# Which of three streams of expert blocks ends in an unfilled step

## The chip, the core and the metric

The kernel runs on one core of one Trainium2 chip. The metric is the device time of one execution in microseconds, here the median of three runs. A profile is one more execution, taken with the hardware profiler on; its span runs from the first instruction to the last.

## The reference, cut to what matters

Two transformer blocks are computed for 512 tokens of width 1024, in float32. The second one ends in a mixture of 32 experts (4 groups of 8). Each token picks its group and the best two experts in it, so there are 1024 assignments of a token to an expert. All of them, whatever their number for one expert, go through that expert's three matrices of 1024x512, 1024x512 and 512x1024:

```python
def hierarchical_moe(h, rg_w, rg_b, re_w, re_b, w_gate, w_up, w_down):
...
    grp = jnp.argmax(group_logits, axis=-1).astype(jnp.int32)
...
    top_val, top_idx = lax.top_k(in_group, TOP_K)
    gate = p_grp * jax.nn.softmax(top_val, axis=-1)
    expert_id = grp[:, None] * EXPERTS_PER_GROUP + top_idx.astype(jnp.int32)
...
    def expert_block(args):
        xb, e = args
        a = xb @ w_gate[e]
        u = xb @ w_up[e]
        return (jax.nn.silu(a) * u) @ w_down[e]
```

The results of a token's two experts are added to it with their gates as weights, and a last normalisation follows.

## The kernel before

The first 1495 us or so are dense layers, attention and a recurrent mixer, and the change touches nothing of them. The router follows, then the experts, then the final gathering and normalisation.

**Blocks and steps.** An expert's assignments are cut into blocks of 32 rows (`BS`). The work on the experts is a chain of steps, one block in each. TensorE does for step c: the gate and up products (`gate_up`, L1760), the transposes of the next step's rows (`next_rows`, L1678), the down product of step c-1 (`down`, L1778) and the transposes of its own products (`turn_products`, L1786). ScalarE and VectorE do the copies and the SiLU in between, GpSimd gathers the rows of later steps, and ScalarE's queue stores each result to `y_rows`.

**Three streams.** Step c belongs to stream c % 3 (`SETS` is 3), and each stream has its own place in SBUF for the three matrices of one expert (`sets`), 3 x 2048 KB. Three steps, one of each stream, are a lap. The number of laps is worked out on the chip, from the routing, and every engine reads it into a register (`laps`). Below, steps count from 0, laps from 0, and the streams are called first, second and third. With the inputs of this case there are 54 steps in 18 laps.

**When weights are loaded.** All loads of weights are issued from SyncE's queue in order of the steps: gate and up of step c once TensorE has ended the gate and up products of step c-3 (`load_first`), and down of step c-1 once the down product of step c-4 is done (`load_down`). A load is conditional (`cond=needed`, L923): the table `need` holds 0 where the stream's next step has the same expert as its last one, and where the step is not filled. So a stream that stays with one expert loads nothing, and an unfilled step loads nothing, though its products are computed all the same, on whatever the buffers hold. Steps 0 to 2 use the experts 0, 1 and 2, whose matrices are loaded before the routing is known.

**How blocks are placed.** The other 29 experts are put in a row, those with the most blocks first, and this row is laid along the first stream from its position 1 to its end, then along the second and then the third. On VectorE this is a sum: `place` is three times the position in that row (`quota` holds the expert's start, `rdiv` the block within the expert), so it is right for the first stream; where it is `turn` or more (three times the number of laps, 54), `shift[:, 0:1]` is added, which moves it into the second stream; where it is `past` or more, `shift[:, 1:2]` is added too, for the third. `heads` holds the blocks of the experts 0, 1 and 2, at least 1 each, `total` all blocks with these, here 53. What is left of the 54 steps is then at the end of the third stream.

**Blocks of this case.** By the reference on the inputs, experts 0 and 1 have one block each and expert 2 none (it still has its step). Of the others, two have 5 blocks, one has 4, two have 3, seven have 2 and sixteen have 1, together 50. So the row is laid like this, each number one expert's blocks, and | the step of the heads:

```
first  stream:  1 | 5 5 4 3                  (17 positions)
second stream:  1 | 3 2 2 2 2 2 2 2          (17)
third  stream:  0 | 1 x 16, and one unfilled (17)
```

The sets of three matrices that laps 1 to 17 load are then 3, 1, 1, 2, 1, 3, 1, 2, 1, 2, 2, 2, 1, 2, 2, 2, 0, together 28. The issues in the trace show this step by step: a transfer that is made takes SyncE's queue 0.33 us or more to issue, one that is left out 0.07 to 0.09 us.

Of the kernel before, what the change touches and what calls it, by code (L numbers as in the profile page):

```python
# [35 lines left out]
SETS = 3  # L36
# [8 lines left out]
ACT, ALU, AX = mybir.ActivationFunctionType, mybir.AluOpType, mybir.AxisListType  # L45
# [83 lines left out]
def build(nc, x_d, cols_d, rows_d, wdense_d, wff_d, wif_d, wr_d, strips_d, experts_d, out_d):  # L129
# [3 lines left out]
    DV = Queue("dv", nc.vector, sem("dve_steps"))  # L133
    PO = Queue("po", nc.gpsimd, sem("pool_steps"))
    SP = Queue("sp", nc.sync, None)
    pe, ac, dv, po, sp = nc.tensor, nc.scalar, nc.vector, nc.gpsimd, nc.sync
# [14 lines left out]
    def sb(name, words, dt=F32, parts=128):  # L151
        return nc.alloc_sbuf_tensor(name, [parts, words], dt)
# [34 lines left out]
    def sm(n):  # L187
        a = small_at[0]
        small_at[0] += n
        assert small_at[0] <= SMALL  # L190
        return small[:, a:a + n]
# [26 lines left out]
    iota_f, tok_id, fold = sb("iota_f", 128), sm(2 * NT), sm(2 * BS)  # L218
# [831 lines left out]
    place = ((2, 0), (3, 0), (2, 0), (3, 384))  # L1050
# [459 lines left out]
    DV.step(dv.tensor_copy(quota[:, 0:3], iota_f[:, 0:3]))  # L1510
    nb, numbers = sm(33), sm(33)
    DV.step(dv.memset(nb[:, 32:33], 0.0))
    DV.step(dv.tensor_copy(numbers[:, 0:32], iota_f[:, 0:32]))
    DV.step(dv.tensor_scalar(numbers[:, 32:33], tok_id[:, 0:1], float(NO_ROW), None, ALU.add))
    DV.step(dv.tensor_scalar(multiples, iota_f[:, 1:T // BS], float(BS), None, ALU.mult))
# [60 lines left out]
    heads, ids1, key, ahead = sm(3), sm(C2), sm(33), sm(1)  # L1576
    pair, total, most, rest, turn = sm(1), sm(1), sm(1), sm(1), sm(1)
    shift, past = sm(2), sm(1)
# [24 lines left out]
    DV.run(dv.tensor_scalar(turn, turn, most, None, ALU.max))  # L1603
    counted_laps = DV.step(dv.tensor_scalar(rest.bitcast(I32), turn, -1.0, None, ALU.add))
    DV.run(dv.tensor_scalar(turn, turn, float(SETS), None, ALU.mult))
    DV.run(dv.tensor_scalar(shift, shift, turn, None, ALU.subtract))
    DV.step(dv.scalar_tensor_tensor(past, turn, 1.0, shift[:, 0:1], ALU.add, ALU.subtract))

    chosen = work[:, 0:2 * NT * 32]
    rank, rdiv, rmod = sm(C2), sm(C2), sm(C2)  # L1610
    place, late, posf, pos = sm(C2), sm(C2), sm(C2), sm(C2)
# [12 lines left out]
                            quota.unsqueeze(1).to_broadcast([128, C2, 32]), ALU.mult))  # L1624
    DV.run(dv.tensor_reduce(place, chosen.rearrange("p (c e) -> p c e", e=32), axis=AX.X, op=ALU.add))
    DV.run(dv.scalar_tensor_tensor(place, rdiv, float(SETS), place, ALU.mult, ALU.add))
    DV.step(dv.tensor_scalar(late, place, turn, shift[:, 0:1], ALU.is_ge, ALU.mult))
    DV.run(dv.tensor_scalar(posf, place, past, shift[:, 1:2], ALU.is_ge, ALU.mult))
    DV.run(dv.tensor_tensor(late, late, posf, ALU.add))
    DV.run(dv.tensor_tensor(place, place, late, ALU.add))  # L1630
# [438 lines left out]
```

How the kernel before makes its waits and increments, by code:

```python
    def run(self, ins):  # L114
        s = self.step(ins)
        self.eng.wait_ge(self.sem, s.value(self.loop))
        return s
# [1 line left out]
    def wait(self, *steps):  # L120
        for s in steps:
            if s is not None:
                self.eng.wait_ge(s.queue.sem, s.value(self.loop))
# [5 lines left out]
def build(nc, x_d, cols_d, rows_d, wdense_d, wff_d, wif_d, wr_d, strips_d, experts_d, out_d):  # L129
# [77 lines left out]
    cleared = PO.run(po.memset(zeros, 0.0))  # L207
    PO.run(po.affine_select(out=ident[:, :], in_=ident[:, :], compare_op=ALU.not_equal, fill=1.0, base=0,
                            pattern=[[-1, 128]], channel_multiplier=1))
    PO.run(po.affine_select(out=tri[:, :], in_=ones[:, :], compare_op=ALU.is_ge, fill=0.0, base=0,
                            pattern=[[1, 128]], channel_multiplier=-1))
    c_ready = PO.run(po.affine_select(out=tri_strict[:, :], in_=ones[:, :], compare_op=ALU.is_gt, fill=0.0,
                                      base=0, pattern=[[1, 128]], channel_multiplier=-1))
    for q in (PE, AC, DV):
        q.wait(c_ready)
        q.eng.wait_ge(s_cols, 16)
    iota_f, tok_id, fold = sb("iota_f", 128), sm(2 * NT), sm(2 * BS)
    PO.run(po.tensor_tensor(fold, ident[:, 0:2 * BS], ident[:, 2 * BS:4 * BS], ALU.add))
    PO.run(po.iota(iota_f[:, :].bitcast(I32), [[1, 128]], base=0, channel_multiplier=0))
# [272 lines left out]
    for k in range(KD):  # L493
        if k % 2 == 0:
            ac.wait_ge(s_x[k // 2], 16)
            dv.wait_ge(s_x[k // 2], 16)
# [32 lines left out]
    dv.wait_ge(s_strip, 16)
    for hh in range(12):
```

## Time and profile before

| | us |
|---|---|
| median of 3 runs | 2052.38 |
| lowest and highest | 2051.47, 2054.06 |
| the profiled execution | 2054.98 |
| its span | 2053.7 |
| SyncE's first conditional load of weights | 1527.21 |
| first loads for step 5 issued (end of lap 0) | 1539.66 |
| first loads for step 53 issued (end of lap 16) | 1994.00 |
| end of the last down product | 2020.33 |

TensorE is busy for 89% of the span. In the stretch of the experts the page's row for the DMA engines is at 9 tenths in slices 31 to 38, with 374 to 415 GB/s, where it stands at 2 or 3 tenths for most of the time before. The laps are cut here at the moment when SyncE issues the first loads for the third stream's next step, which is when TensorE has ended the third stream's gate and up products of that lap. Such a lap lasts 21.2 us where nothing waits, 7.07 us for a step.

### The profile page before, as it was taken

The page shows a single profiled execution, that of the slowest core. Times are in us where ns is not written, and L with a number is a line of the kernel's source. Part 1 is how long each engine was busy: PE and PEld are TensorE (multiplying, and loading weights), DVE is VectorE, ACT ScalarE, POOL GpSimd, SP SyncE. Part 2 cuts the span into 40 slices and gives each one's busy share as a digit, 9 for nine tenths or more (in the row PEclk, how much of TensorE's full clock was granted, in tenths as well). Part 3 has the DMA queues.
Part 4 walks back from the last instruction along what each step waited for, and adds up shares of the span by engine and source line. Part 5 has one row for each costly group of instructions (what it writes and reads, how often), then busy time and mean ns, then how long its engine had stood idle before and what let it go on. Part 6 is the DMA issues. An engine that isn't in the chain of part 4 may idle for free.

```text
span 2053.7 us, 27415 instructions
## 1 busy us (share of the span) xinstructions
PE 1824.7 (89%) x9686; PEld 1287.1 (63%) x9686; DVE 863.6 (42%) x1256; ACT 432.7 (21%) x794; POOL 992.7 (48%) x536
## 2 busy tenths in 40 slices
PE   5999999989999899999999798996877978969783
PEld 4888888877776578888888666664642423323331
DVE  5444443410254567444444489877341111111113
ACT  3111100100244432111100143551321211111112
POOL 5888887767544278888888523321211111101101
PEclk9999999999999999999999999997868988988897
DMA  3333363423221123333333222210579999999983
GB/s 126 97 97 93 105 262 98 141 79 98 66 62 52 32 85 95 97 93 101 92 109 98 72 60 64 72 52 21 212 287 412 374 408 402 410 415 398 413 358 133
DMA packets 56977, 346.00 MB, mean 168 GB/s; under 512 B 8474, under 2 KB 8858, under 8 KB 44896
## 3 DMA queue, kind: packets, MB, share of 16 engines
q1 hardware_dynamic: 44640, 315.12, 42.1%
q10 hardware_dynamic: 7968, 19.46, 2.6%
q0 software_dynamic: 4320, 10.78, 1.5%
q8 instruction: 29, 0.48, 0.1%
q14 instruction: 20, 0.16, 0.0%
HBM read 475.06 MB, written 19.66 MB: 241 GB/s over the span
## 4 chain that ended last, share of the span: by engine, by line
PE 70%; DMA 13%; DVE 11%; ACT 3%; issue 1%; POOL 1%; SPq 0%; DVEq 0%; ACTq 0%; POOLq 0%
PE bank L460 31%; DMA big<-w_up_in 13%; PE bank L431 12%; PE bank L1760 7%; PE bank L692 4%; PE bank L1266 3%; DVE big L1043 3%; PE bank L1778 2%; PE bank L479 2%; PE bank L1376 2%; PE bank L1786 1%; PE bank L610 1%; DVE state L1028 1%; PE bank L670 1%; PE bank L1678 1%
## 5 line engine op out<-in xcount | busy, mean ns | idle before, releaser
L277 POOL TENSOR_TENSOR weights_hi_parts<-ring,ones 128x1024 fp32r<-128x1024 f32 (+1 forms) x176 | 356.6, 2026 | 304.7 <-PE bank L460 139.1
L279 POOL TENSOR_TENSOR ring_parts<-ring,weights_hi_parts 128x1024 fp32r<-128x1024 f32 (+1 forms) x176 | 473.9, 2693 | 13.8
L460 PE MATMUL bank<-attention_buffers_parts,weights_hi_parts 128*128 128x512 f32 x832 | 329.4, 396 | 27.9 <-POOL ring_parts L279 17.6
L460 PE MATMUL bank<-state_parts,weights_hi_parts 128*128 128x512 f32 x832 | 326.8, 393 | 0.0
L460 PE MATMUL bank<-attention_buffers_parts,ring_parts 128*128 128x512 f32 x832 | 326.7, 393 | 0.0
L1760 PE MATMUL bank<-big,work 128*32 128x512 f32 x1440 | 231.7, 685 | 54.5 <-DMA big<-w_up_in 54.4
L431 PE MATMUL bank<-big_parts,weights_hi_parts 128*128 128x512 f32 x704 | 217.1, 389 | 1.2 <-POOL ring_parts L279 1.2
L460 PEld LDWEIGHTS bank<-attention_buffers_parts,weights_hi_parts 128*128 128x128 f32 x832 | 158.1, 190 | 64.6 <-POOL ring_parts L279 17.6
L864 POOL TENSOR_TENSOR ring_parts<-ring,weights_hi_parts 128x1024 fp32r<-128x1024 f32 x32 | 81.0, 2534 | 234.1 <-ACT weights_hi_parts L861 234.1
L1860 POOL TENSOR_TENSOR small<-small 128x1 f32<-128x1 f32 x51 | 9.7, 190 | 381.3 <-DVE small L1683 381.3
L460 PEld LDWEIGHTS bank<-state_parts,weights_hi_parts 128*128 128x128 f32 x832 | 158.3, 190 | 33.4 <-issue 0.8
L460 PEld LDWEIGHTS bank<-attention_buffers_parts,ring_parts 128*128 128x128 f32 x832 | 158.0, 190 | 33.5
L1719 DVE TENSOR_TENSOR work<-bank,cols 128x256 f32<-128x256 f32 x54 | 22.9, 425 | 306.0 <-PE bank L1678 304.9
L431 PEld LDWEIGHTS bank<-big_parts,weights_hi_parts 128*128 128x128 f32 x704 | 132.0, 188 | 29.2 <-POOL ring_parts L279 2.0
L1760 PEld LDWEIGHTS bank<-big,work 128*32 128x32 f32 x1440 | 63.6, 123 | 135.3 <-issue 129.6
L431 PE MATMUL bank<-big_parts,ring_parts 128*128 128x512 f32 x352 | 136.9, 389 | 0.0
L406 DVE TENSOR_TENSOR work<-bank,token_scale 128x512 f32<-128x512 f32 x44 | 30.4, 692 | 199.9 <-PE bank L460 199.9
L1043 DVE SCALAR_TENSOR_TENSOR big<-big,cols 128x512 f32<-128x512 f32 x120 | 106.5, 929 | 6.4 <-ACT big L1037 5.3
L315 DVE TENSOR_TENSOR big_parts<-work,big_parts 128x512 f32 (+1 forms) x44 | 82.9, 1884 | 42.3 <-ACT big_parts L313 42.3
L1792 ACT ACTIVATE weights_hi<-bank 128x512 f32<-128x512 f32 x54 | 32.3, 598 | 312.1 <-PE bank L1760 312.1
L1760 PE MATMUL bank<-attention_buffers,work 128*32 128x512 f32 x288 | 75.0, 667 | 24.0 <-DMA big<-w_up_in 23.4
L313 ACT ACTIVATE big_parts<-work 128x512 f32 (+1 forms) x44 | 27.9, 633 | 287.3 <-DVE work L408 287.3
(377 smaller groups left out, 2827.1 us busy)
## 6 DMA issues: line engine op xcount, KB each, us to landing
big<-w_up_in SPq DMA_DIRECT2D x54, 2048.0 KB
ring<-wdense_in SPq DMA_DIRECT2D x176, 512.0 KB, 3.6
state<-w_down_in SPq DMA_DIRECT2D x37, 2048.0 KB
big<-w_gate_in SPq DMA_DIRECT2D x36, 2048.0 KB
attention_buffers<-w_gate_in SPq DMA_DIRECT2D x18, 2048.0 KB
ring<-w_down_in SPq DMA_DIRECT2D x18, 2048.0 KB
ring<-wff_in SPq DMA_DIRECT2D x32, 704.0 KB, 4.1
y_rows<-big ACTq DMA_DIRECT2D x1, 8192.0 KB, 28.0
```

The costliest lines, as they stand in the source:

```text
L277: po.tensor_tensor(hi, raw, ones[:, 0:1].to_broadcast([128, words]), ALU.mult).then_inc(PO.sem, 1)
L279: po.tensor_tensor(lo, raw, hi.bitcast(F32), ALU.subtract) \
L315: return DV.step(dv.tensor_tensor(lo, raw, hi.bitcast(F32), ALU.subtract))
L431: m = pe.matmul(bank, x, y_, start=t + k + n == 0, stop=t == 1 and k == h - 1 and n == 2)
L460: m = pe.matmul(out, x, y_, start=j + n == 0, stop=j == len(pairs) - 1 and n == len(ts) - 1)
L479: m = pe.matmul(banks[t][:, :], x, y_, start=k + n == 0, stop=k == KD - 1 and n == len(ts) - 1)
L692: m = pe.matmul(banks[7][:, :], x, y_, start=k + t == 0, stop=k == KD - 1 and t == 2, skip_group_check=True)
L864: lo_made[n] = PO.step(po.tensor_tensor(lo, raw, hi.bitcast(F32), ALU.subtract))
L1043: last = DV.step(dv.scalar_tensor_tensor(dst, src, w, dst, ALU.mult, ALU.add))
L1266: m = pe.matmul(banks[bank][:, :], x, y_, start=k + j == 0, stop=k == KD - 1 and j == 2, skip_group_check=True)
L1376: m = pe.matmul(bank[:, :], x, y_, start=k == 4 and n == 0, stop=k == 3 and n == 2, skip_group_check=True)
L1760: m = pe.matmul(first_products[b][p:p + BS, :], xet[:, (k + odd) * BS:(k + odd + 1) * BS], sets[b][m_][:, (k + odd) * D_EXP:(k + odd + 1) ...
```

## The change

One step of the row, or two, that no block fills are moved: with one unfilled step it is the last of the first stream, and with two they are the last of the first and of the second. Before they were the last of the third. `room` holds three times the number of positions that the first and the second stream have, and takes the place of `turn` in `shift`, `past` and `late`. `spare` is a new constant (1, 2), which becomes 1 or 0 for "at least one (two) unfilled". `room` is never less than three times the blocks of that stream's head.

```diff
@@ -1510,6 +1510,8 @@
     DV.step(dv.memset(nb[:, 32:33], 0.0))
+    spare, room = sm(2), sm(2)
+    DV.step(dv.tensor_copy(spare, iota_f[:, 1:3]))
     DV.step(dv.tensor_copy(numbers[:, 0:32], iota_f[:, 0:32]))
@@ -1603,8 +1605,12 @@
     DV.run(dv.tensor_scalar(turn, turn, float(SETS), None, ALU.mult))
-    DV.run(dv.tensor_scalar(shift, shift, turn, None, ALU.subtract))
-    DV.step(dv.scalar_tensor_tensor(past, turn, 1.0, shift[:, 0:1], ALU.add, ALU.subtract))
+
+    DV.run(dv.tensor_scalar(spare, spare, total, turn, ALU.add, ALU.is_le))
+    DV.run(dv.tensor_scalar(spare, spare, -float(SETS), turn, ALU.mult, ALU.add))
+    DV.run(dv.scalar_tensor_tensor(room, heads[:, 0:2], float(SETS), spare, ALU.mult, ALU.max))
+    DV.run(dv.tensor_tensor(shift, shift, room, ALU.subtract))
+    DV.step(dv.scalar_tensor_tensor(past, room[:, 1:2], 1.0, shift[:, 0:1], ALU.add, ALU.subtract))
@@ -1624,7 +1630,7 @@
-    DV.step(dv.tensor_scalar(late, place, turn, shift[:, 0:1], ALU.is_ge, ALU.mult))
+    DV.step(dv.tensor_scalar(late, place, room[:, 0:1], shift[:, 0:1], ALU.is_ge, ALU.mult))
```

`run` is a step after which the engine waits for its end; `step` has no such wait. On VectorE, in the routing, the kernel before has these rows, where `small` is the buffer in which `turn`, `shift`, `past` and `rest` are columns:

```order
 L1603 TENSOR_SCALAR small<-small 128x1
 L1604 TENSOR_SCALAR small<-small 128x1
 L1605 TENSOR_SCALAR small<-small 128x1
 L1606 TENSOR_SCALAR small<-small 128x2
 L1607 SCALAR_TENSOR_TENSOR small<-small 128x1
 L1614 TENSOR_TENSOR work<-small,bank 128x256
```

and the changed kernel has these in the same place:

```order
 L1605 TENSOR_SCALAR small<-small 128x1
 L1606 TENSOR_SCALAR small<-small 128x1
 L1607 TENSOR_SCALAR small<-small 128x1
 L1609 TENSOR_SCALAR small<-small 128x2
 L1610 TENSOR_SCALAR small<-small 128x2
 L1611 SCALAR_TENSOR_TENSOR small<-small 128x2
 L1612 TENSOR_TENSOR small<-small 128x2
 L1613 SCALAR_TENSOR_TENSOR small<-small 128x1
 L1620 TENSOR_TENSOR work<-small,bank 128x256
```

Three small operations have come in between the number of laps and the placing of the blocks. The copy for `spare` (L1514) stands earlier, among the constants. No other engine has a row more or less, or in another place: the loops are the same, and what differs in them is the contents of the tables (which expert and which rows a step has, and which loads are left out).

## Rows read from the trace of the kernel before

**Rows 1.** The page, the span in 40 slices: gigabytes per second moved by DMA.
```profile
GB/s 126 97 97 93 105 262 98 141 79 98 66 62 52 32 85 95 97 93 101 92 109 98 72 60 64 72 52 21 212 287 412 374 408 402 410 415 398 413 358 133
```
**Rows 2.** SyncE's queue: start, duration, line, what it loads, times.
```profile
1967.38 0.33 SPq L923 DMA_DIRECT2D big<-w_gate_in  x1
...
1974.45 0.09 SPq L923 DMA_DIRECT2D attention_buffers<-w_gate_in  x1
...
1976.91 0.34 SPq L923 DMA_DIRECT2D state<-w_down_in  x1
...
1994.00 0.07 SPq L923 DMA_DIRECT2D big<-w_gate_in  x1
```
**Rows 3.** Windows, laps 1 to 14, one row each; columns in the first line.
```profile
core 0: us, PE busy (x) PEld busy (x) DVE busy (x) ACT busy (x) POOL busy (x), PEclk, DMA share, GB/s
1539.66:1580.57 40.91, 26.23 (x195) 10.71 (x194) 4.24 (x12) 4.41 (x10) 3.31 (x6) 0.79 1.01 415
1580.57:1601.78 21.21, 21.21 (x195) 8.68 (x194) 4.24 (x12) 4.41 (x10) 3.34 (x6) 1.00 0.93 359
1601.78:1622.98 21.20, 21.20 (x195) 8.67 (x194) 4.24 (x12) 4.41 (x10) 3.31 (x6) 1.00 0.96 368
1622.98:1650.03 27.05, 22.86 (x195) 9.96 (x194) 4.24 (x12) 4.41 (x10) 3.34 (x6) 0.94 1.02 414
1650.03:1671.23 21.20, 21.20 (x195) 8.66 (x194) 4.24 (x12) 4.40 (x10) 3.31 (x6) 1.00 1.01 400
1671.23:1716.79 45.56, 27.95 (x195) 11.40 (x194) 4.23 (x12) 4.41 (x10) 3.34 (x6) 0.74 1.01 417
1716.79:1738.00 21.21, 21.21 (x195) 8.68 (x194) 4.24 (x12) 4.41 (x10) 3.31 (x6) 1.00 0.98 377
1738.00:1765.48 27.48, 23.09 (x195) 9.91 (x194) 4.24 (x12) 4.41 (x10) 3.34 (x6) 0.94 1.01 413
1765.48:1786.69 21.21, 21.21 (x195) 8.68 (x194) 4.23 (x12) 4.41 (x10) 3.31 (x6) 1.00 1.01 410
1786.69:1815.88 29.19, 24.01 (x195) 9.53 (x194) 4.24 (x12) 4.40 (x10) 3.34 (x6) 0.88 1.01 410
1815.88:1853.47 37.59, 26.91 (x195) 9.96 (x194) 4.24 (x12) 4.41 (x10) 3.31 (x6) 0.77 1.01 415
1853.47:1880.48 27.01, 24.20 (x195) 9.34 (x194) 4.23 (x12) 4.40 (x10) 3.34 (x6) 0.87 0.99 411
1880.48:1901.69 21.21, 21.21 (x195) 8.67 (x194) 4.24 (x12) 4.41 (x10) 3.31 (x6) 1.00 0.97 377
1901.69:1929.78 28.09, 24.68 (x195) 10.69 (x194) 4.24 (x12) 4.40 (x10) 3.34 (x6) 0.88 1.01 410
```
**Rows 4.** TensorE's timeline: start, duration, line, operation, times, the idle time before it.
```profile
1644.78 4.93 PE L1760 MATMUL bank<-big,work 128*32 128x512 f32 x32 [4.10 <-DMA big<-w_up_in]
...
1988.36 5.34 PE L1760 MATMUL bank<-big,work 128*32 128x512 f32 x32 [3.23 <-DMA big<-w_up_in]
...
2011.26 3.64 PE L1760 MATMUL bank<-big,work 128*32 128x512 f32 x32
...
2018.41 1.92 PE L1778 MATMUL bank<-state,weights_hi 128*32 128x512 f32 x16 [0.76 <-DVE weights_hi L1830]
```
**Rows 5.** Windows where the transfers end, columns as in rows 3.
```profile
1992.00:1994.00 2.00, 2.00 (x22) 0.69 (x15) 0.00 (x0) 0.25 (x1) 0.00 (x0) 0.95 1.02 434
1994.00:1995.00 1.00, 1.00 (x13) 0.48 (x16) 0.47 (x2) 0.35 (x1) 0.00 (x0) 1.00 0.43 180
1995.00:1996.00 1.00, 1.00 (x12) 0.13 (x4) 0.00 (x0) 0.00 (x0) 0.00 (x0) 1.00 0.16 66
```
**Rows 6.** VectorE's timeline in the routing: start, duration, line, operation, form.
```profile
1506.61 0.27 DVE L1597 TENSOR_SCALAR small<-small 128x1 f32<-128x1 f32 x1
...
1507.87 0.14 DVE L1605 TENSOR_SCALAR small<-small 128x1 f32<-128x1 f32 x1
1508.05 0.23 DVE L1606 TENSOR_SCALAR small<-small 128x2 f32<-128x2 f32 x1
1508.31 0.16 DVE L1607 SCALAR_TENSOR_TENSOR small<-small 128x1 f32<-128x1 f32 x1
```

## The prediction, made before the changed kernel ran

> **What bounds the kernel now.** I read the page's slices first: in slices 31 to 38 DMA moves 374 to 415 GB/s, against mostly 60 to 110 before [rows 1]. That is where the experts run, so the question is whether TensorE or the transfers set the pace there. The windows cut at laps answer it [rows 3]. In a lap with one set of weights TensorE is busy for all of its 21.2 us at a granted clock of 1.00. In a lap with two or three sets it is not (22.9 to 28.0 us busy of 27.0 to 45.6), its clock falls to 0.74 to 0.94, and DMA moves 410 to 417 GB/s with a share of about 1. The timeline of TensorE shows the waits: a step's gate and up products start after an idle time that the landing of `w_up` ends [rows 4]. So the bound is the transfers, in all laps but those with one set, and even there 359 to 410 GB/s flow, of what earlier laps left over. A set is 3 x 2048 KB = 6.29 MB, 15.2 us at 415 GB/s. Besides it a lap moves 0.8 MB of gathered rows and stored results (3 x 0.13 MB each way), 1.9 us.
>
> **What the change does to the sets.** The unfilled step exists: at 1994.00 the loads for step 53 are left out (0.07 us), where those of steps that load take 0.33 us and more [rows 2]. It goes to step 51. The first stream then holds 16 positions after its head, 5 5 4 2; the second 17, 1 3 2 2 2 2 2 2 1; the third 17, 1 and 1 x 16. Before, the two boundaries between streams fell between experts. Now one expert with three blocks and one with two are cut in two, and each is loaded in both streams. Sets in laps 1 to 17:
>
> before: 3 1 1 2 1 3 1 2 1 2 2 2 1 2 2 2 0, together 28
> after: 3 2 1 1 2 2 2 1 2 1 3 1 2 1 3 1 2, together 30
>
> Two costs and one gain follow: 12.6 MB more through a full queue, and a last step that has to wait for its weights; but the weights now end with the last step instead of three steps before it.
>
> **Sum by the laps.** Laps of the same sets in the same streams, with a like history, exist in the trace [rows 3], so I put the new sequence together from them. The window before them (up to 1539.66) is unchanged but for the routing.
> Lap 1, three sets: as it was, 40.9.
> Lap 2, two sets (second and third stream) behind a lap of three: not in the trace. Below.
> Laps 3 and 4, one each: 2 x 21.2 = 42.4.
> Laps 5 to 9, sets 2 2 2 1 2: these are laps 10 to 14 of before, stream by stream, 29.2 + 37.6 + 27.0 + 21.2 + 28.1 = 143.1. Lap 5 comes behind two laps of one set, as lap 4 did (27.05 instead of 29.19), so 2.1 less: 141.0.
> Laps 10 to 14, sets 1 3 1 2 1: laps 5 to 9 of before, 21.2 + 45.6 + 21.2 + 27.5 + 21.2 = 136.7.
> Laps 15 to 17, sets 3 1 2: laps 6 to 8 of before, 45.6 + 21.2 + 27.5 = 94.2.
> From the end of step 53's gate and up products to the end of its down product: 5.5, from 2014.9 to 2020.3 [rows 4]. Its down weights should not be late: in the last waited step of before, the products began at 1988.36, the rate fell from 434 to 180 GB/s in the window from 1994 [rows 5], so the last weights were there some 6 us later, and the down product would want its weights 8.9 us after the start (2011.26 to 2018.41, and 5.34 instead of 3.64 for the products) [rows 4].
>
> For lap 2 I count bytes. In the kernel before, lap 2 needed 6.3 + 0.8 MB and moved 359 x 21.2 = 7.6 MB, so 0.5 MB were left over from lap 1. Now gate and up of step 7 (4.2 MB) were asked for in lap 1 as well, into a queue that was full, so 4.7 MB are left. Gate and up of step 8, the rest of the lap's traffic, and perhaps down of step 7 are ahead of step 8's products: 4.7 + 4.2 + 0.8 = 9.7 MB, or 11.8 MB with it; 23.4 or 28.4 us. The same count for lap 4 of before gives 20.4 or 25.5, and step 14's products began 21.8 us after the lap's start (1644.78 - 1622.98) [rows 3, 4], so I take 1.4 above the lower figure, 24.8, and 5.5 for the products at a fallen clock (4.93 and 5.34 are rows) [rows 4]: 30.3. The ends are 27.0, the shortest lap of two sets here, and 37.6, the longest [rows 3].
>
> Sum: 40.9 + 30.3 + 42.4 + 141.0 + 136.7 + 94.2 + 5.5 = 491.0, against 2020.3 - 1539.7 = 480.7 before. That is 10.3 more.
>
> **The same by the queue, as a check.** Two sets more: 2 x 15.2 = 30.3. The end: before, the last down product ended at 2020.3, 25.9 us after the weights had ended (1994.4, from the 180 GB/s of a window of 1 us) [rows 4, 5]; after, products that begin 6 us before that point need 5.34 + 5.5 = 10.8, so 4.8 remain, 21.1 less (three steps of 7.07). The queue's slack: the six laps of one set fell short of 415 GB/s by 2.9, 2.4, 0.8, 1.9, 0.3 and 1.9 us (each 21.2 x (1 - rate/415)), 10.2 in all [rows 3]; there will be seven such laps, so 1.7 more. 30.3 - 21.1 + 1.7 = 10.9. The two ways agree.
>
> The page "DMA: Bandwidth & Descriptors" of the Trainium skill, section "Specifications", lists about 358 GB/s as the HBM limit of one core; this case's trace differs, with 410 to 417 GB/s in every lap that waits [rows 3], and I go by the trace. By the page's figure a set would be an estimated 17.6 us, and the queue's sum 4.8 us higher.
>
> **The routing.** Three operations more stand in a chain in which each waits for the one before. Their like take 0.18 to 0.30 us from start to start (L1605 to L1606 0.18, L1606 to L1607 0.26; L1597, with two scalars from memory as the new comparison has, lasts 0.27) [rows 6]. I take 0.7 us, all on the path, since the first gather and so the first products wait for the tables; hidden it is 0, at most 0.9. The constant `spare` is one operation of some 0.1 us before the logits are there, hidden by the wait for them.
>
> **Forecast.** 10.3 + 0.7 = 11.0 us more. The profiled execution took 2054.98 us, its span and 1.3 us around it, and 2.6 more than the median of the runs; the difference goes onto the median: 2052.4 + 11.0 = 2063.4.
>
> **Rivals.**
> (a) The waits cost more than their bytes. In lap 2 both loading streams wait, as in the two laps of 37.6 us, and lap 5 is 29.2. TensorE's clock is 0.74 to 0.79 in laps of three sets [rows 3], and products that end later ask for the next weights later. Price 7.3 + 2.1: 20.4 more, 2072.8. For it speaks that the sequence changes between one and three sets more often; against it, that the share of DMA stays about 1 in all such laps.
> (b) The queue's slack takes up part of the sets. If all 10.2 us of it are used, 30.3 - 10.2 - 21.1 + 0.7 = -0.3: 2052.1, no change. Against it: a stream cannot load ahead by more than its own next expert, and laps 3 and 4 come with one set each.
> (c) The end decides, and the kernel gets faster. The two sets land beside computation early on, so that laps 2, 5 and 7 are laps of 21.2 us (9.1 + 5.8 + 5.8 less), and the 21.1 us at the end remain as a gain: 11.0 - 20.7 = -9.7, 2042.7. It decides from the point where the queue brings the 13 sets and 7 x 0.8 MB of laps 1 to 7, 87 MB, in 40.9 + 5 x 21.2 + 37.6 = 184.5 us. That needs 474 GB/s, and the highest rate in a window here is 434 [rows 5].
> (d) The steps stay as they are, because the count of blocks fills them all and step 53 only kept its expert. Then only the routing is longer: 2053.1. Against it: the third stream changes its expert in every lap up to 16.
>
> **How the numbers follow.** The forecast has 0.78, (a) 0.10, (b) 0.07, (c) 0.03, (d) 0.02. The forecast's own spread: with lap 2 at 27.0 it is 7.7 more, 2060.1; with lap 2 at 33 and lap 5 at 29.2 it is 15.8, 2068.2; runs differ by 1 to 2 us besides. The range is 2058 to 2070; (a)'s full price, (b), (c) and (d) are outside. A measurement tells about 0.2%, 4.1 us, from no change. Slower by more: 0.88; within: (b) and (d), 0.09; faster: 0.03.
>
> **What would show it.** In the profile after: 90 transfers of weights from L923 that are made (30 sets), and 12.6 MB more in SyncE's queue; the loads for step 51 left out and those for 53 made; lap 2 of about 30 us, laps 11 and 15 of about 45, laps 3, 4, 8, 10, 12, 14 and 16 at 21.2; the last down product some 5 us after the weights end, instead of 26, and at about 2031. The forecast is wrong if single laps are longer than 21.2, if the rate in waiting laps is not near 415, or if step 53's down product waits for its weights.

## The result, and the profile after

| | before | changed |
|---|---|---|
| median of 6 runs, us | 2054.14 | 2062.29 |
| lowest and highest | 2051.47, 2054.59 | 2060.42, 2063.68 |
| the profiled execution, its span | 2054.98, 2053.7 | 2063.64, 2062.4 |

The ratio of the changed kernel to the one before is 1.0044, with a 95% interval of 1.0034 to 1.0054: slower by 9.0 us (7.0 to 11.1), or by 8.2 from median to median. The forecast was 11.0 more, at 2063.4, in a range of 2058 to 2070. In the experiments below one run took 2527 us (experiment 4) and one of the kernel before 6310 us; no ratio uses either.

The sets did what the table of the blocks says. The page's row for SyncE's queue has 327.70 MB, where before has 315.12: 12.58 MB more, two sets. SyncE's timeline of the changed kernel (start, duration, line, what it loads), from step 51's loads on:

```profile
1983.61 0.09 SPq L923 DMA_DIRECT2D attention_buffers<-w_gate_in  x1
1983.80 0.07 SPq L923 DMA_DIRECT2D big<-w_up_in  x1
...
1990.67 0.34 SPq L923 DMA_DIRECT2D big<-w_gate_in  x1
1991.11 0.40 SPq L923 DMA_DIRECT2D big<-w_up_in  x1
...
1997.74 0.33 SPq L923 DMA_DIRECT2D big<-w_gate_in  x1
1998.17 0.38 SPq L923 DMA_DIRECT2D big<-w_up_in  x1
```

Step 51's loads are left out (0.09 and 0.07 us), steps 52 and 53 load (0.33 us and more). Before, the last was left out [rows 2]. The windows of the changed kernel cut at the same moments as [rows 3], for laps 1 to 4, 6, 11, 15, 16, and lap 17 to the end of its products:

```profile
core 0: us, PE busy (x) PEld busy (x) DVE busy (x) ACT busy (x) POOL busy (x), PEclk, DMA share, GB/s
1541.84:1580.96 39.12, 27.16 (x195) 11.56 (x194) 4.24 (x12) 4.40 (x10) 3.30 (x6) 0.83 1.01 413
1580.96:1610.67 29.71, 22.82 (x195) 10.18 (x195) 4.23 (x12) 4.41 (x10) 3.33 (x6) 0.89 1.01 412
1610.67:1632.95 22.28, 21.29 (x195) 8.77 (x195) 4.23 (x12) 4.40 (x10) 3.30 (x6) 1.00 0.96 387
1632.95:1654.15 21.20, 21.20 (x195) 8.67 (x194) 4.24 (x12) 4.41 (x10) 3.33 (x6) 1.00 0.97 378
...
1682.70:1720.15 37.45, 25.93 (x195) 9.71 (x194) 4.23 (x12) 4.40 (x10) 3.33 (x6) 0.82 1.01 413
...
1817.18:1861.10 43.92, 26.43 (x195) 11.26 (x194) 4.24 (x12) 4.41 (x10) 3.30 (x6) 0.81 1.01 416
...
1931.13:1976.54 45.41, 27.23 (x195) 10.10 (x194) 4.23 (x12) 4.42 (x10) 3.30 (x6) 0.77 0.98 408
1976.54:1997.74 21.20, 21.20 (x195) 8.66 (x194) 4.24 (x12) 4.41 (x10) 3.33 (x6) 1.00 0.97 379
...
1997.74:2020.96 23.22, 20.95 (x189) 8.46 (x187) 4.24 (x12) 4.16 (x9) 0.00 (x0) 1.00 1.01 429
```

Lap 2, two sets where before had one, lasts 29.7 us instead of 21.2. Besides lap 1, the laps of three sets are 11 and 15 now, and they last 43.9 and 45.4 us. In all laps of two or three sets the rate is 408 to 423 GB/s, near the 410 to 417 of before [rows 3].

The end of TensorE's timeline (idle time before a row in brackets), and the windows in which the weights end:

```profile
2017.32 3.64 PE L1766 MATMUL bank<-big,work 128*32 128x512 f32 x32 [2.27 <-DMA big<-w_up_in]
2022.55 1.92 PE L1784 MATMUL bank<-state,weights_hi 128*32 128x512 f32 x16 [1.59 <-DMA state<-w_down_in]
2024.40 1.10 PE L1792 MATMUL bank<-small,weights_hi 128*128 128x64 f32 x8
2027.56 1.92 PE L1784 MATMUL bank<-state,weights_hi 128*32 128x512 f32 x16 [2.05 <-DMA state<-w_down_in]
```

```profile
2024.00:2025.00 1.00, 1.00 (x12) 0.60 (x6) 0.00 (x0) 0.47 (x1) 0.00 (x0) 1.00 1.04 442
2025.00:2026.00 1.00, 0.51 (x5) 0.37 (x4) 0.79 (x2) 0.40 (x2) 0.00 (x0) 1.00 0.43 180
2026.00:2028.00 2.00, 0.44 (x4) 0.16 (x8) 0.14 (x1) 0.00 (x0) 0.00 (x0) 1.00 0.27 72
```

The last down product ends at 2029.5, 4.1 us after the fall of the rate (2025.4), which is taken here as the end of the weights; before it was 25.9 us [rows 4, 5]. It and the down product before it wait for their weights, 2.05 and 1.59 us, which no down product near the end did in the kernel before.

### The profile page after: what moved, and what is told of

Read it like the earlier page. It is cut to its first block, busy times and chain, and to the rows that moved or that the text cites. A ratio compares the mean times of both kernels' runs of the same rounds, so it can differ in the third digit from the quotient of the medians.

```text
span 2062.4 us, 27419 instructions
## 1 busy us (share of the span) xinstructions
PE 1822.6 (88%) x9686; PEld 1286.5 (62%) x9686; DVE 864.1 (42%) x1260; ACT 432.7 (21%) x794; POOL 992.1 (48%) x536
## 3 DMA queue, kind: packets, MB, share of 16 engines
q1 hardware_dynamic: 45504, 327.70, 43.3%
## 4 chain that ended last, share of the span: by engine, by line
PE 69%; DMA 14%; DVE 11%; ACT 3%; issue 1%; POOL 1%; SPq 0%; DVEq 0%; ACTq 0%; POOLq 0%
PE bank L460 31%; PE bank L431 12%; DMA big<-w_up_in 9%; PE bank L1766 6%; DMA state<-w_down_in 5%; PE bank L692 4%; PE bank L1266 3%; DVE big L1043 3%; PE bank L1784 3%; PE bank L479 2%; PE bank L1376 2%; PE bank L1792 1%; PE bank L610 1%; DVE state L1028 1%; PE bank L670 1%
## 5 line engine op out<-in xcount | busy, mean ns | idle before, releaser
L277 POOL TENSOR_TENSOR weights_hi_parts<-ring,ones 128x1024 fp32r<-128x1024 f32 (+1 forms) x176 | 356.5, 2026 | 305.1 <-PE bank L460 139.4
L460 PE MATMUL bank<-attention_buffers_parts,weights_hi_parts 128*128 128x512 f32 x832 | 329.4, 396 | 27.9 <-POOL ring_parts L279 17.6
L313 ACT ACTIVATE big_parts<-work 128x512 f32 (+1 forms) x44 | 27.9, 633 | 287.3 <-DVE work L408 287.3
L1825 DVE TENSOR_TENSOR ring<-bank,work 64x512 f32<-64x512 f32 x53 | 36.2, 683 | 121.6 <-ACT work L1808 121.6
```

Of the source, the lines that this page charges most:

```text
L277: po.tensor_tensor(hi, raw, ones[:, 0:1].to_broadcast([128, words]), ALU.mult).then_inc(PO.sem, 1)
L460: m = pe.matmul(out, x, y_, start=j + n == 0, stop=j == len(pairs) - 1 and n == len(ts) - 1)
```

## The experiments

Each run is compared with runs of the kernel before on the same chip, 2054.08 us in the first four experiments and 2053.46 us in the others. Differences between two medians are given beside the ratios where that is plainer. The laps are read from one profiled execution of each kernel, and they differ a little between executions: of the laps that load the same in the kernel before and in experiment 1, lap 8 lasted 27.5 and 29.0 us, lap 12 27.0 and 25.1.

**1. The three operations alone.**

```diff
-    DV.step(dv.tensor_copy(spare, iota_f[:, 1:3]))
+    DV.step(dv.tensor_copy(spare, iota_f[:, 4:6]))
```

> The changed kernel with the constants 4 and 5 instead of 1 and 2 in spare, so that no step is ever taken for unfilled and the blocks stand where they stood before: the three operations alone. Theory (the routing is on the path, the queue starts with it): 0.7 us more than before, about 2054.8. Rival (what the profile of the changed kernel shows at the start counts in full: lap 0 ended 2.2 us later, because the products of step 0 took 1.3 us longer at a lower clock): 2.2 us more. Second rival (the full queue of the first laps takes it up): 0.

Measured: 2053.93 us, ratio 1.0006 (0.9996 to 1.0016). Nothing that can be measured; the interval, -0.8 to 3.3 us, excludes none of the three. The trace shows how far the 2.1 us get by which lap 0 ends later (1541.75, as in the changed kernel). Step 5's products, the last of lap 1, wait for their weights in both kernels; before and here they begin at:

```profile
1574.15 6.11 PE L1760 MATMUL bank<-big,work 128*32 128x512 f32 x32 [7.17 <-DMA big<-w_up_in]
1574.90 5.73 PE L1766 MATMUL bank<-big,work 128*32 128x512 f32 x32 [7.09 <-DMA big<-w_up_in]
```

That is 0.75 us later, about what the three operations take, and not 2.1: the rival of 2.2 us has no support here. Lap 1 ends 0.4 us later (1580.95), because these products took less time. The last down product ends at 2020.1, where before it is 2020.3, but behind sixteen more laps that vary as said above this does not tell 0.7 from 0.

**2. Two sets more, and nothing else.** In the kernel before:

```diff
     tables = DV.run(dv.scalar_tensor_tensor(need[:, SETS:SLOT_COLS].bitcast(I32), exp1[:, SETS:SLOT_COLS], 0.0, changed,
                                             ALU.is_gt, ALU.mult))
+    tables = DV.run(dv.memset(need[:, 9:10].bitcast(I32), 1))
+    tables = DV.run(dv.memset(need[:, 21:22].bitcast(I32), 1))
```

> The kernel before, with the table of needed loads set to 1 at steps 9 and 21 (first stream, laps 3 and 7), where the stream keeps its expert: two sets are loaded a second time, 30 sets with the blocks and the end of before. This is the price of two sets by itself. Theory (full queue, 15.2 us a set, less the slack of the two laps of one set in which they fall, 2.4 and 1.9 us): 26 to 30 us more, 2080 to 2084. Rival (the slack of all laps of one set, 10.2 us, takes its part): 20 more, 2074. Rival (each wait costs its cold clock besides): 33 or more, 2087.

Measured: 2079.34 us, 25.3 more; ratio 1.0136 (1.0121 to 1.0151), which is 27.9 us. The profiled execution came to the experts 8 us or more earlier than any other here (lap 0 ended at 1530.84, before at 1539.66), in the part that no kernel of this study touches, so its laps are read by themselves. Laps 3 and 7, which had been laps of 21.2 us:

```profile
1591.34:1624.98 33.64, 22.96 (x195) 9.32 (x194) 4.24 (x12) 4.41 (x10) 3.30 (x6) 0.90 1.01 413
1717.00:1754.66 37.66, 25.02 (x195) 9.54 (x194) 4.24 (x12) 4.40 (x10) 3.30 (x6) 0.77 1.01 413
```

They cost 12.4 and 16.5 us more, and the queue is full in both (413 GB/s). From the end of lap 0 to the end of the last down product it is 24.4 us more than before, since other laps came out shorter. By the ratio's interval, 24.9 to 31.0 us, the theory's 26 to 30 holds, 20 and 33 do not; by the medians it is a little too high.

**3. The unfilled step at the end of the second stream.**

```diff
-    DV.step(dv.tensor_copy(spare, iota_f[:, 1:3]))
+    DV.step(dv.tensor_copy(spare[:, 0:1], iota_f[:, 2:3]))
+    DV.step(dv.tensor_copy(spare[:, 1:2], iota_f[:, 1:2]))
```

> The changed kernel with the constants 2 and 1 in spare, so that the one unfilled step is the last of the second stream: one expert is cut in two, 29 sets. By the sum of the laps: laps 1 to 16 load what they load in the kernel before, and lap 17 loads one set instead of none, which a lap of 21.2 us hides; so only the routing is left, 0.7 us more than before, 2054.8. By the sum of the queue (one set more 15.2, the end 21.1 shorter, routing 0.7): 5 us less, 2049. The two sums agreed for the change itself and part here.

Measured: 2054.42 us, ratio 1.0003 (0.9994 to 1.0012). The sum by the laps is right and the sum by the queue is wrong. Laps 16 and 17 of this kernel:

```profile
1970.26:1997.02 26.76, 24.04 (x195) 9.30 (x194) 4.24 (x12) 4.40 (x10) 3.34 (x6) 0.87 0.96 400
1997.02:2018.00 20.98, 20.98 (x193) 8.54 (x195) 4.24 (x12) 4.18 (x10) 0.00 (x0) 1.00 0.84 326
```

Lap 17 brings a set now, and TensorE is busy all the same (20.98 of 20.98 us). In the kernel before, that lap's queue brought no weights. Laps 1 to 16, which load the same sets in both, take 455.0 us here and 454.3 before. So the 25.9 us behind the last weights were not a tail that waited to be cut: they were a lap of computation that has to be done in any case, and that can hide a set.

**4. The unfilled step behind the head of the third stream.** In the kernel before:

```diff
+    DV.step(dv.tensor_scalar(pair, turn, total, float(SETS), ALU.subtract, ALU.mult))
     DV.run(dv.tensor_scalar(shift, shift, turn, None, ALU.subtract))
+    DV.run(dv.tensor_tensor(shift[:, 1:2], shift[:, 1:2], pair, ALU.add))
```

> The kernel before, with three times the number of unfilled steps added to the second column of shift (two operations more): the unfilled step stands right behind the head of the third stream, as step 5, and its blocks end with step 53. No expert is cut: 28 sets. By the sum of the laps: lap 1 has two sets instead of three (27 to 29 us instead of 40.9, or the queue's 15.2 less), laps 2 to 16 as before, lap 17 one set, hidden: 12 to 15 us less than before, 2039 to 2042. By the sum of the queue (no set more, the end 21.1 shorter): 2033.5. Rival (the place of the unfilled step gains nothing, only the cut experts cost): 2054.

Measured: 2044.45 us, ratio 0.995 (0.993 to 0.997), which is 4 to 14 us less; five of the six runs lie from 2035 to 2047. This is the fastest kernel here of those that load every set they compute with: by the medians 9.6 us less than the one before, 17.8 less than the changed one. The estimate by the laps, 2039 to 2042, was 2 to 5 us too good, the one by the queue 11. Laps 1, 16 and 17:

```profile
1539.13:1569.16 30.03, 25.03 (x195) 11.03 (x194) 4.24 (x12) 4.41 (x10) 3.30 (x6) 0.89 0.90 359
...
1956.91:1981.97 25.06, 22.74 (x195) 9.06 (x194) 4.24 (x12) 4.41 (x10) 3.33 (x6) 0.93 1.01 424
1981.97:2003.00 21.03, 21.03 (x193) 8.54 (x195) 4.24 (x12) 4.22 (x10) 0.00 (x0) 1.00 0.86 333
```

Lap 1 loads two sets and lasts 30.0 us instead of 40.9, at 359 GB/s: part of the gain is given back as slack of the queue, since the third stream's next weights (step 8) are asked for only when the unfilled step's products end, at 1569.16. From 1566 on DMA moves 43 GB/s:

```profile
1566.00:1569.16 3.16, 3.16 (x34) 1.04 (x27) 0.00 (x0) 0.26 (x1) 0.00 (x0) 1.00 0.18 43
```

The set that was moved from lap 1 to lap 17 costs nothing there.

**5. Two sets less, in the laps of three.** In the changed kernel:

```diff
+    tables = DV.run(dv.memset(need[:, 34:35].bitcast(I32), 0))
+    tables = DV.run(dv.memset(need[:, 46:47].bitcast(I32), 0))
```

> The changed kernel with the loads for steps 34 and 46 left out (second stream, laps 11 and 15, the two laps of three sets); these steps and those that follow with the same expert compute with the weights of the expert before. 28 sets, and the end of the changed kernel. Theory (a set in a full queue costs its bytes, and in its own lap): 15 us less in each of the two laps, 2062.3 - 30.3 = 2032. By the price of the sets that the added loads showed (25.3 us for two): 2037. Rival (laps with a first-stream load cost 37.5 us, whatever else they load): 6 and 8 us less, 2048.

Measured: 2042.19 us, 20.1 less than the changed kernel. All three expectations miss: 30 and 25 are too much, 14 too little. The two laps:

```profile
1816.63:1850.45 33.82, 22.77 (x195) 9.29 (x194) 4.24 (x12) 4.40 (x10) 3.29 (x6) 0.90 0.90 366
1919.31:1955.16 35.85, 25.49 (x195) 9.87 (x194) 4.23 (x12) 4.41 (x10) 3.30 (x6) 0.86 0.88 357
```

They are 10.1 and 9.6 us shorter, and now the queue has slack in them: 366 and 357 GB/s, which against 415 is 4.0 and 5.0 us left unused. A set taken from a full queue gives its 15.2 us only as long as the queue stays full.

**6. The changed kernel without its last cut.** `need` is 0 at step 52, in the same manner.

> The changed kernel with the load for step 52 left out (second stream, lap 17, the second half of the expert that is cut there); its step computes with the weights of the expert before. Sum by the laps: lap 17 has one set, which 21.2 us hide as in the run with the unfilled step in the second stream (23.2 in the changed kernel), and the last down product comes 5.5 us after the last gate and up products instead of 8.6: 5 us less than the changed kernel, 2057. Sum by the queue: 15.2 less, 2047.

Measured: 2057.16 us, 5.1 less than the changed kernel. The sum by the laps said 5, the sum by the queue 15. The last down product waits for VectorE alone again, as in the kernel before:

```profile
2020.94 1.92 PE L1785 MATMUL bank<-state,weights_hi 128*32 128x512 f32 x16 [0.76 <-DVE weights_hi L1837]
```

**7. The changed kernel without the added set of lap 2.** `need` is 0 at step 7.

> The changed kernel with the load for step 7 left out (second stream, lap 2, behind the cut expert's last block in lap 1); steps 7, 10 and 13 compute with the weights of the expert before. Sum by the laps: lap 2 is a lap of one set, 21.2 instead of 29.7, and lap 3 21.2 instead of 22.3: 9.6 less than the changed kernel, 2052.7. Sum by the queue: 15.2 less, 2047.

Measured: 2053.99 us, 8.3 less than the changed kernel. By the two ratios, 0.9995 (0.9986 to 1.0004) and 1.0044, it is 10.1 less. The sum by the laps said 9.6, the sum by the queue 15. Laps 2 and 3, which in the changed kernel last 29.7 and 22.3 us:

```profile
1581.30:1602.50 21.20, 21.20 (x195) 8.66 (x194) 4.24 (x12) 4.40 (x10) 3.34 (x6) 1.00 0.94 359
1602.50:1623.70 21.20, 21.20 (x195) 8.66 (x194) 4.24 (x12) 4.41 (x10) 3.30 (x6) 1.00 0.88 328
```

**8. The changed placing without cuts.** In the changed kernel, behind the table `numbers`:

```diff
+    DV.wait(DV.now())
+    for e, up in ((7, 80.0), (4, 38.0)):
+        DV.step(dv.tensor_scalar(numbers[:, e:e + 1], numbers[:, e:e + 1], -up, None, ALU.add))
+        DV.run(dv.scalar_tensor_tensor(numbers[:, 32:33], ident[:, e:e + 1], -up, numbers[:, 32:33], ALU.mult, ALU.add))
```

> The changed kernel with two experts moved in the row (one of two blocks in front of those with three, one of one block in front of the last with two), so that the boundaries fall between experts again: first stream 5 5 4 2 and the unfilled step, second 3 3 2 2 2 2 2 1, third 2 and fifteen 1, 28 sets; four small operations more among the constants. Sets by lap: 3 0 1 2 1 2 2 1 2 1 3 1 2 1 3 1 2. Sum by the laps, with those of the changed kernel: 39.1 + 2 x 21.2 + 27 + 21.2 + 37.5 + 27 + 21.6 + 28.7 + 21.2 + 43.9 + 21.2 + 27.2 + 21.6 + 45.4 + 21.2 + 23.2 + 8.6 = 478 after the end of lap 0, 9.7 less than the changed kernel and 2.7 less than the one before: 2052. Sum by the queue (no set more, the end 21.1 shorter): 2034. If only the cuts made the change slower, and its end a gain of 21 us, it is the second.

Measured: 2051.39 us, ratio to the kernel before 0.9989 (0.998 to 0.9998): 2.3 us less (0.4 to 4.1), where the sum by the laps said 2.7 less. The weights end with the last step here, no set is added, and the gain is 2 us and not 21. TensorE's last row shows what stands against it, a wait for the last down weights:

```profile
2017.46 2.77 PE L1788 MATMUL bank<-state,weights_hi 128*32 128x512 f32 x16 [2.91 <-DMA state<-w_down_in]
```

## Why the prediction came out right, point by point

**The table of the sets** was right in every step: 30 sets in the laps that it named, step 51 left out.

**The number** was nearer than the reasoning. The median came out 1.1 us under the forecast of 2063.4, but the forecast stood on a median of 3 runs, 2052.38, and all 6 runs of the kernel before give 2054.14. The forecast difference, 11.0, was 2 to 3 us too large.

**The sum by the laps** was right in size, and its terms one by one, against what the changed kernel's profile shows:

| stretch | forecast | measured |
|---|---|---|
| later end of lap 0 | 0.7 | 2.2 |
| lap 1 | 40.9 | 39.1 |
| lap 2 | 30.3 | 29.7 |
| laps 3 and 4 | 42.4 | 43.5 |
| laps 5 to 9 | 141.0 | 141.8 |
| laps 10 to 14 | 136.7 | 135.2 |
| laps 15 to 17 | 94.2 | 89.8 |
| products of step 53 to the end of its down product | 5.5 | 8.5 |

The total is 489.8 us with the start, where 491.7 was forecast and the kernel before has 480.7. Two terms were off by more than 2 us, both at the end, and that they offset each other (4.4 us less, 3.0 more) is luck.

Lap 17 was put at 27.5 us, as lap 8 of before, and lasted 23.2. Its last products began 19.6 us after the lap's start and took 3.64 us at full clock; those of lap 8 before began after 21.8 us, behind a longer wait, and took 5.34:

```profile
1759.83 5.34 PE L1760 MATMUL bank<-big,work 128*32 128x512 f32 x32 [3.81 <-DMA big<-w_up_in]
```

Lap 17 gathers no more rows (POOL 0.00 in its window) and its rate is 429 GB/s, in lap 8 before 413 [rows 3]. Whether the missing gathers are the cause of the earlier weights was not tried.

And I said that step 53's down product would not wait. It did, and so did step 52's. The products began 8.1 us before the rate fell (2017.3 and 2025.4) instead of the 6 I took, and ran 3.64 us instead of 5.34, so the down product wanted its weights sooner. But the larger part is another: I took the fall of the rate for the arrival of the weights, and the wait ended only at 2027.5, 2.1 us later, with some traffic still running (72 GB/s in the window from 2026). In the kernel before nothing waited for these last weights, so no row of its end shows this. That is 3.0 us more.

**Lap 2** was right by two errors that nearly cancel. Step 8's products were put 24.8 us behind the lap's start and at 5.5 us, as products at a fallen clock. They began 25.8 us behind it and took 3.64; it was step 7's products, before them, that ran at the fallen clock:

```profile
1596.90 5.12 PE L1766 MATMUL bank<-big,work 128*32 128x512 f32 x32 [5.68 <-DMA big<-w_up_in]
...
1606.72 3.64 PE L1766 MATMUL bank<-big,work 128*32 128x512 f32 x32 [1.21 <-DMA big<-w_up_in]
...
1611.97 0.64 PE L1784 MATMUL bank<-state,weights_hi 128*32 128x512 f32 x4 [0.99 <-DMA state<-w_down_in]
```

The last row is in lap 3: a down product waits 0.99 us for lap 2's added set, and that lap lasts 22.3 us instead of 21.2.

**The signs of being wrong.** Three were named. The rate held, at 408 to 423 GB/s in the laps of two and three sets. Of the seven single laps four lasted 21.2 us and three a little more (laps 3, 8 and 14: 22.3, 21.6 and 21.6), which is 1.9 us together. The third came in full: step 53's down product waited for its weights, so the step "its down weights should not be late" was wrong.

**The end of the span.** From the last down product to the end of the span it is 32.9 us, and 33.4 before.

**The routing.** The three operations took what was said, 0.7 us. From L1607 to L1613 it is 1.16 us (1507.94 to 1509.10), where before has 0.44 from L1605 to L1607 [rows 6]. VectorE's timeline of the changed kernel:

```profile
1507.94 0.14 DVE L1607 TENSOR_SCALAR small<-small 128x1 f32<-128x1 f32 x1
1508.12 0.29 DVE L1609 TENSOR_SCALAR small<-small 128x2 f32<-128x2 f32 x1
1508.45 0.23 DVE L1610 TENSOR_SCALAR small<-small 128x2 f32<-128x2 f32 x1
1508.71 0.16 DVE L1611 SCALAR_TENSOR_TENSOR small<-small 128x2 f32<-128x2 f32 x1
1508.90 0.16 DVE L1612 TENSOR_TENSOR small<-small 128x2 f32<-128x2 f32 x1
1509.10 0.16 DVE L1613 SCALAR_TENSOR_TENSOR small<-small 128x1 f32<-128x1 f32 x1
```

Whether they lie on the path to the end is left open: in experiment 1 the products that end lap 1 begin 0.75 us later, as they would if the 0.7 us were on the path, but the ratio of the times, 1.0006 with an interval of -0.8 to 3.3 us, does not tell 0.7 from 0.

**The sum by the queue**, given as a check, agreed to 0.6 us (10.9 and 10.3) and for the wrong reason. It had 30.3 us for two sets and 21.1 us for the end. The experiments give the two added sets 8.3 and 5.1 us (7 and 6), and the end without them a gain of 2 (8), or of 5 when both are taken from the changed kernel's time (2062.3 - 8.3 - 5.1 = 2048.9, against 2054.1; this takes it that the two prices add). Both gross terms were two to ten times too large, and the errors cancelled. Its error is in the step "the end: 21.1 less": the queue is not full in the last lap before, and a set that moves into it costs nothing, but it also ends nothing sooner, because the three steps have to be computed. Experiment 3 separates the two sums plainly, with 0.3 us measured, 0.7 and -5 expected.

**The rivals.** (a) did not come: lap 2 was 29.7 and not 37.6. (b), with 2052.1, and (c), with 2042.7, are far from the 2062.3 measured; they priced the queue's slack over the whole stretch; what the slack takes depends on the lap, all of a set in lap 17 (3), little in laps 3 and 7 (2). (d) was wrong: step 51's loads are left out and step 53's are made.

**The page's rate.** "DMA: Bandwidth & Descriptors" of the Trainium skill, section "Specifications", lists about 358 GB/s; the changed kernel's laps of two and three sets ran at 408 to 423 GB/s, and the measurement decides.

## What to carry to other kernels

Where an engine and a queue take turns as the bound, price a change by laps with the same history and not by bytes over the whole stretch: one set of 6.29 MB, 15.2 us of queue, cost 12 to 17 us added to laps 3 and 7, which already loaded one; 8 to 11 us in lap 2 and in the laps of three; 5 us as the second set of the last lap; and nothing as the only set of the last lap, where the queue brought no other weights. Do not take a fall of the transfer rate for the moment at which an engine that waits for the data goes on: here it was 2.1 us later. A second sum that agrees with the first is no check if it has large terms of both signs; find a case in which the two part, and run that. Of the three other places tried for the unfilled step, the ends of the first and the second stream and behind the head of the third, the last gained 10 us, since there it stands in lap 1, which had three sets and a full queue; the end of the first stream gained 2 us where no expert was cut, and the end of the second nothing. How places in other laps compare was not tried.

## What the runs showed of the hardware

The granted clock of TensorE at the start of the experts came back later by more than the work before it did. The windows of the kernel before and of the kernel with the three operations alone (experiment 1), each from about the start of step 0's products, columns as above:

```profile
1521.98:1524.00 2.02, 2.02 (x12) 0.59 (x16) 0.00 (x0) 0.00 (x0) 1.12 (x2) 0.50 0.73 280
1524.00:1527.00 3.00, 3.00 (x27) 0.70 (x20) 0.00 (x0) 0.05 (x1) 0.00 (x0) 0.91 1.03 363
...
1524.50:1525.00 0.50, 0.50 (x12) 0.15 (x8) 0.00 (x0) 0.00 (x0) 0.00 (x0) 0.94 0.47 156
```

```profile
1522.87:1525.00 2.13, 2.13 (x12) 0.49 (x16) 0.00 (x0) 0.00 (x0) 1.10 (x2) 0.50 0.75 298
1525.00:1529.00 4.00, 4.00 (x26) 0.85 (x18) 0.00 (x0) 0.00 (x0) 0.00 (x0) 0.63 1.02 353
...
1527.50:1528.00 0.50, 0.50 (x8) 0.11 (x4) 0.00 (x0) 0.00 (x0) 0.00 (x0) 0.54 0.79 303
```

Step 0's products began 0.8 us later (1521.98 and 1522.77) and were followed by the next transposes 2.1 us later (1526.81 and 1528.89), because most of them ran at 0.50, which is 1.2 GHz: the granted clock reached 1.00, 2.4 GHz, just after 1524.5 in the one kernel and just before 1528 in the other. The changed kernel's profile shows the same. Of the 2.1 us, 0.75 are left where step 5's products begin, as experiment 1 shows. Why the clock came back later was not tried.
